# Three transformer blocks on one core: side stages at other positions, and the last changes of line by halves of the tokens

## The reference, cut to what matters

```python
def third_block(x, c, w_ada, b_ada, norm1_g, w_in, ..., w_out, norm2_g, w_ff1, w_ff2, final_g):
    ...
        xn = modulate(rmsnorm(h, norm1_g[l]), sh1, sc1)
        p = xn @ w_in[l]
        y_a = gmlp_branch(...)                  # token mixing, 8 groups
        y_b = mlstm_branch(...)                 # 4 heads of 256, called the memory here
        merged = sigmoid(p[GA]) * y_a + sigmoid(p[GB]) * y_b
        h = h + g1[:, None, :] * (merged @ w_out[l])
        xn = modulate(rmsnorm(h, norm2_g[l]), sh2, sc2)
        ff = jnp.square(jax.nn.relu(xn @ w_ff1[l])) @ w_ff2[l]      # 1024 -> 4096 -> 1024
        h = h + g2[:, None, :] * ff
    return rmsnorm(h, final_g)
```

## Time and profile before

| what | value |
|---|---|
| median of 3 runs (lowest, highest) | 2628.07 us (2627.79, 2630.12) |
| the profiled execution: its time | 2626.06 us |
| its span in the trace | 2624.2 us |
| TensorE busy | 2519.7 us (96%), 15220 matmuls |
| VectorE busy | 1540.4 us (59%) |
| ScalarE busy | 1084.1 us (41%) |
| GpSimd busy | 328.2 us (13%) |
| granted TensorE clock, mean | 0.991 |

### The profile page before, as it was taken

How to read it: one execution, slowest core, us unless ns; L and a number is a source line. 1 busy time by engine, 2 the same in 40 slices (tenths; PEclk the granted TensorE clock), 3 DMA queues, 4 the chain that set the end, 5 groups by cost and what they waited for, 6 DMA issues and landing times.

```text
span 2624.2 us, 37785 instructions
## 1 busy us (share of the span) xinstructions
PE 2519.7 (96%) x15220; PEld 2077.0 (79%) x15220; DVE 1540.4 (59%) x2544; ACT 1084.1 (41%) x1949; POOL 328.2 (13%) x225
## 2 busy tenths in 40 slices
PE   8889899999999999999899999999999999999998
PEld 6778898999998877766577777878866777699886
DVE  4987754654445457476647787454744544676444
ACT  4465454543223253235642223254333333466323
POOL 0143210012222010000012222020000000500001
PEclk9999999999999999999999999999999999999999
DMA  4211122222323341520035664332221123233332
GB/s 172 85 54 49 57 65 65 81 89 89 95 90 89 97 145 49 175 74 2 1 105 188 206 195 134 96 105 88 81 73 56 49 89 96 73 105 105 99 95 72
DMA packets 76987, 244.91 MB, mean 93 GB/s; under 512 B 12708, under 2 KB 18213, under 8 KB 76558
## 3 DMA queue, kind: packets, MB, share of 16 engines
q1 hardware_dynamic: 69470, 215.72, 26.6%
q10 hardware_dynamic: 7344, 26.77, 3.1%
HBM read 238.25 MB, written 6.90 MB: 93 GB/s over the span
## 4 chain that ended last, share of the span: by engine, by line
PE 78%; DVE 12%; ACT 5%; issue 3%; POOL 2%; DMA 0%; SPq 0%; ACTq 0%; DVEq 0%; POOLq 0%
PE ps L659 51%; PE ps L2525 8%; PE ps L861 5%; DVE wl L392 2%; ACT wh L380 2%; PE ps L3252 2%; PE ps L3961 1%; PE ps L3052 1%; PE ps L2273 1%; DVE xl L1126 1%; PE ps L2301 1%; DVE arena L1527 1%; PE ps L2290 1%; DVE arena L3631 1%; PE ps L1231 1%
## 5 line engine op out<-in xcount | busy, mean ns | idle before, releaser
L659 PE MATMUL ps<-xh,wh 128*128 128x512 f32 (+1 forms) x2536 | 932.4, 383 | 23.7 <-DVE xl L1152 8.1
L659 PE MATMUL ps<-xl,wh 128*128 128x512 f32 (+1 forms) x2536 | 913.5, 376 | 0.0
L659 PE MATMUL ps<-xh,wl 128*128 128x512 f32 (+1 forms) x2536 | 909.6, 374 | 0.0
L392 DVE TENSOR_TENSOR wl<-ring,wh 128x1024 fp32r<-128x1024 f32 x362 | 461.7, 1276 | 483.8 <-ACT wh L380 483.0
L380 ACT ACTIVATE wh<-ring 128x1024 fp32r<-128x1024 f32 x360 | 380.4, 1057 | 822.3 <-PE ps L659 726.8
L659 PEld LDWEIGHTS ps<-xh,wh 128*128 128x128 f32 x2536 | 464.5, 189 | 143.9 <-issue 41.9
L659 PEld LDWEIGHTS ps<-xh,wl 128*128 128x128 f32 x2536 | 464.1, 190 | 89.1
L659 PEld LDWEIGHTS ps<-xl,wh 128*128 128x128 f32 x2536 | 463.1, 189 | 88.2 <-issue 5.5
L2525 PE MATMUL ps<-xh,wh 128*128 128x264 f32 (+1 forms) x816 | 254.2, 312 | 5.3 <-DVE xl L446 3.8
L1221 POOL TENSOR_TENSOR arena<-arena 128x512 f32<-128x512 f32 (+1 forms) x35 | 60.3, 1727 | 1557.9 <-ACT arena L1206 1557.9
L2525 PE MATMUL ps<-xl,wh 128*128 128x264 f32 (+1 forms) x816 | 233.6, 286 | 0.0
(11 more groups left out here) (424 smaller groups left out, 3203.8 us busy)
## 6 DMA issues: line engine op xcount, KB each, us to landing
ring<-in_weights SPq DMA_DIRECT2D x374, 512.0 KB, 3.6
arena<-in_w_ada ACTq DMA_DIRECT2D x48, 512.0 KB, 4.5
arena<-in_cmp_w SPq DMA_DIRECT2D x2, 2048.0 KB
strip_copies<-strip_scratch SPq DMA_DIRECT2D x8, 327.5 KB, 6.3
arena<-strip_copies SPq DMA_DIRECT2D x8, 264.0 KB, 4.0
out_features<-arena SPq DMA_DIRECT2D x8, 256.0 KB, 2.1
token_scratch<-arena SPq DMA_DIRECT2D x3, 512.0 KB, 6.4
arena<-token_scratch SPq DMA_DIRECT2D x12, 128.0 KB, 4.0
```

What stands on the lines that cost most here:

```text
L392: dve.tensor_tensor(flat(self.wl[:, s % 2]), flat(self.ring[:, s % RING]), flat(self.wh[:, s % 2]).bitcast(F32), ALU.subtract).then_inc(se ...
L659: last = pe.matmul(self.place(u, e), w[:, k, :], x[:, k, o:o + m], start=(k == 0 and i == 0), stop=(k == self.chunks - 1 and i == 2))
```

## The change

It has two parts. The first gives other numbers to the positions of side stages in all three blocks, and nothing else: no instruction is added or taken away. The second is in block 3. The last two units (6 and 7) of the line behind `w_out` and of the last line are computed by halves of the tokens: first tokens 0 to 255 of both, then tokens 256 to 511 of both, the second half into another bank. `HalvedSums` makes the root for each half (squares of the last two chunks, ones, Ln and Exp by halves), `HalvedNorm` norms the first half while TensorE still works on the second, and the first two units of `Squared` (`opening`) go by halves too, unit 1 a few chunks behind unit 0. `Final` works and stores by halves: 16 operations and stores of 256 tokens instead of 8 of 512. `Squared` has eleven pairs instead of twelve, from unit 8 on instead of 6, and its planned start is 0.259 units behind the line before it, not 2.5.

Of the first part, three places of some fifty (the planner of block 1, and the memory):

```diff
-                    x.exp.append(x.mask[m] + 0.15 + 0.05 * m)
+                    x.exp.append(x.mask[m] + 0.167 + 0.05 * m)
...
                 free = x.keep[-1:] + [last.out for a in (1,) if s]
-                x.turned.append(max([x.turn + 0.27 * x.width * e, done + 0.15] + [a + 0.1 for a in free]))
+                x.turned.append(max([x.turn + 0.307 * x.width * e, done + 0.238] + [a + 0.048 for a in free]))
...
-            x.weigh = max(x.turn + 0.62 * x.width, x.keep[-1] + 0.12)
...
+            x.weigh = max(x.turn + 0.637 * x.width, x.keep[-1] + 0.116)
...
-        return self.at + 3 * (n // 4) + 0.6 * (n % 4)
+        return self.at + 2.8 * (n // 4) + 0.6 * (n % 4)
...
     memory = Memory(core, 31.2, QK[:, 0:NC], QK[:, NC:2 * NC], VT, EB, QK[:, 0:NC], PT, N, hsq, hr, conv, gates, tokens,
-                    (38, 40, 42.5, 45.3))
+                    (37.42, 40.3, 42.5, 45.13))
```

The second part:

```diff
-        if both:
+        end = self.n - 2 if self.halved else self.n
+        if self.opening:
+            for e in range(2):
+                lag = OPENING_LAG[e]
+                for k in range(NC + lag):
+                    if k < NC:
+                        yield 0, k, e
+                    if k >= lag:
+                        yield 1, k - lag, e
...
+        yield from [(u, k, None) for u in range(2 if both or self.opening else 0, end) for k in chunks if not self.paired(u)]
+        if self.halved:
+            yield from [(u, k, e) for e in range(2) for u in (self.n - 2, self.n - 1) for k in chunks]
...
+    def tensor(self, pe):
+        for e in range(2):
+            yield self.end(e) + (0.48 if e else 0.111)
+            got = self.core.ps[:, self.bank, e * HALF:e * HALF + HALF]
+            if e:
+                pe.wait_ge(self.root.sem, self.root.at(1))
+            for n, a in enumerate((self.acc, self.sq[:, (NC - 2) % 2], self.sq[:, (NC - 1) % 2])):
+                if n == 0:
+                    pe.wait_ge(self.added.sem, self.added.at(NC - 3))
+                else:
+                    pe.wait_ge(self.squared.sem, self.squared.at(NC - 2 + 2 * e + n))
+                last = pe.matmul(got, self.core.c("ones"), a[:, e * HALF:e * HALF + HALF], start=(n == 0), stop=(n == 2))
+            last.then_inc(self.summed.sem, 1)
...
+    def vector(self, dve):
+        for e in range(2):
+            a = self.half(e)
+
+            def part(k):
+                dve.wait_ge(self.hi.sem, self.hi.at(NC * e + k + 1))
+                dve.scalar_tensor_tensor(out=self.core.xl[:, k, a], in0=self.kept[:, k, a], scalar=self.shifts[k],
+                                         in1=self.core.xh[:, k, a].bitcast(F32), op0=ALU.add, op1=ALU.subtract).then_inc(self.lo.sem, 1)
+            for k in range(NC):
+                yield self.begin[e] + 0.145 * k
+                if k == 0:
+                    dve.wait_ge(self.sums.root.sem, self.sums.root.at(e + 1))
+                if k >= 2:
+                    part(k - 2)
+                dve.scalar_tensor_tensor(out=self.kept[:, k, a], in0=self.tiles[k][:, a], scalar=self.gains[k], in1=self.sums.r[:, a],
+                                         op0=ALU.mult, op1=ALU.mult).then_inc(self.made.sem, 1)
...
+            yield self.begin[1] + 0.145 * (k + 2) + 0.2
+            pool.wait_ge(self.lo.sem, self.lo.at(NC + k + 1))
+            pool.tensor_scalar(self.kept[:, k], self.kept[:, k], self.shifts[k], None, ALU.add).then_inc(self.shifted.sem, 1)
...
     def vector(self, dve):
-        yield self.sums.end() + 1
-        dve.wait_ge(self.sums.root.sem, self.sums.root.at(1))
-        for k in range(NC):
-            dve.scalar_tensor_tensor(out=self.final[:, k], in0=self.tiles[k], scalar=self.gains[k], in1=self.sums.r,
-                                     op0=ALU.mult, op1=ALU.mult).then_inc(self.made.sem, 1)
+        for e in range(2):
+            a = slice(e * HALF, e * HALF + HALF)
+            for k in range(NC):
+                yield self.sums.end(e) + 0.543 + 0.001 * k
+                if k == 0:
+                    dve.wait_ge(self.sums.root.sem, self.sums.root.at(e + 1))
+                dve.scalar_tensor_tensor(out=self.final[:, k, a], in0=self.tiles[k][:, a], scalar=self.gains[k], in1=self.sums.r[:, a],
+                                         op0=ALU.mult, op1=ALU.mult).then_inc(self.made.sem, 1)
...
+    def vector_half(self, dve, u, e):
+        dve.wait_ge(*((self.core.used, self.first + u + 1) if e else (self.half.sem, self.half.at(u - NC + 3))))
+        a = slice(e * HALF, e * HALF + HALF)
+        out = self.tiles[u][:, a]
+        dve.scalar_tensor_tensor(out=out, in0=self.place_half(u, e), scalar=self.scale[u], in1=out, op0=ALU.mult,
+                                 op1=ALU.add).then_inc(self.free.sem, 1)
...
-    last = Added(core, at, WHOLE, four, inputs, NC, h, cols(2 * NC))
+    last = Added(core, at, WHOLE, four, inputs, NC, h, cols(2 * NC), halved=(0, 1))
     last.alone = NC // 2
-    sums = Sums(core, at, 1, h, last.ready, T, 4, tmp, norm, names)
-    inputs_2 = Normed(core, h, at + NC + 1.1, sums.root, norm, cols(4 * NC), cols(3 * NC), 0, columns_ready, core.area(2 * NC * T, NC, T))
-    at += NC + 2.5
+    sums = HalvedSums(core, last, h, 4, tmp, norm, names)
+    inputs_2 = HalvedNorm(core, h, (at + NC - 0.75, at + NC + 1.213), sums, cols(4 * NC), cols(3 * NC), core.area(2 * NC * T, NC, T))
+    at += NC + 0.259
     three = (0, 1, 2)
-    up = Squared(core, 4 * NC, at, three, inputs_2, hidden, (6, 12))
-    up.alone = 0
-    of_norm = Quadrants(core, at + 1.6, inputs_2.kept, inputs_2.ready, hi, lo, quarters(3 * NC * T, 4))
+    up = Squared(core, 4 * NC, at, three, inputs_2, hidden, (8, 11))
+    up.opening = True
+    of_norm = Quadrants(core, at + 2.944, inputs_2.kept, inputs_2.ready, hi, lo, quarters(3 * NC * T, 4), split=(0.787,0.733))
...
-    some, last, at = down(core, at + up.start(4 * NC), up, hidden, 4 * NC, h, three, cols(5 * NC), quadrants=quadrants)
-    sums = Sums(core, last.at, last.d, h, last.ready, T, 4, 0, core.area(3 * T, T), names, ends=last.ends())
+    some, last, at = down(core, at + up.start(4 * NC), up, hidden, 4 * NC, h, three, cols(5 * NC), quadrants=quadrants, halved=(2, 3))
+    sums = HalvedSums(core, last, h, 4, 0, core.area(3 * T, T), names)
```

More of the change, by code:

```diff
@@ L1422, in down @@
         inputs = Inputs(core, [hidden[:, g + k] for k in range(m)], at - last.d, SEQ, ready=ready)
-        before = Added(core, at, WHOLE, banks, inputs, m, tiles, scale, pairs)
+        before = Added(core, at, WHOLE, banks, inputs, m, tiles, scale, pairs, halved if g + NC >= n else ())
         stages += [inputs, before]
@@ L3964, in steps @@
         def steps():
-            yield self.when(0) - 0.35
+            yield self.when(0) - 0.41
             score(0)
```

253 lines of the change are left out of this document (175 added, 78 removed).

## The result

The changed kernel took 2600.09 us (median; 2596.42 to 2605.73), the kernel before 2629.1 on the same chip; the ratio is 0.9888 (95% interval 0.9874 to 0.9903), that is 29 us. The forecast was 2616, in a range from 2607 to 2624. It had the sign right and the term of the halves, and fell short by some 17 us of gain, nearly all of it from the moved positions. A second measurement (`e8_all_again`) gave 2599.46 and 0.9887 (0.9869 to 0.9904).

A forecast was written before the change was run, and what follows sets the result against it. TensorE, carrying 78% of the chain, was taken to bound the kernel. Positions 8.0 plus halves 3.8 saved 11.8 us from the profiled 2626.06, giving 2614.3; 2.0 for the median made 2616, range 2607 to 2624.

The forecast's parts named there:

- Part B: The halves in block 3: change of line, pairs and tail together save 3.8 us.
- rival 4: Block 3's halves: the weight load sets their pace, 0.188 us each, 20 us more, 2636 us; chance 0.02.
- 2.5 - 1.1 - 0.6 = 0.8: Block 3's lines: 2.5 us saved at the change of line, 1.1 lost by eleven pairs, 0.6 by splitting wholes.
- Part A: The moved positions in all three blocks: 3.5 + 1.0 + 3.5 = 8.0 us saved.
- 1.6 + 1.4 + 2.0 - 1.5 = 3.5: Block 1, us saved: weighing waits 1.6, sums of squares 1.4, turns 2.0, less 1.5 for lost cover in differential heads.
- "1.0" of block 2: Block 2's scan and attention steps: 1.0 us saved, bounds 4 saved and 3 lost.
- the 3.5 of the mixer: Block 3's mixer: masked-score waits 3.0 us and two short ones 1.1 saved, less 0.6 for new waits.
- Cover: Other TensorE matmuls between a side chain's start and the instruction needing its result, at 0.12 us per 256-column matmul.
- Rival 1: Larger gain: change-of-line clock 1.5 us, block 2 3 more, block 1 4 more; 2607.5 us; chance 0.2.
- Rival 2: Change of line gives nothing, VectorE bounding it before and after; 2620.5 us; chance 0.15.
- Rival 3: Moved positions give nothing, TensorE waiting at the next instruction instead; saving falls from 8 to 1, 2623 us; chance 0.1.
- Rival 5: Slower: side work ahead of weight splits on VectorE makes TensorE wait; 25 units with 1 us each give 2629; chance 0.02.

The follow-up runs named there:

- e5_planner: Only the new numbers of block 1's attention planner, the rest as in the kernel before; ratio 0.9997 (0.9982 to 1.0012).
- e13_means_diff: The kernel before with block 1's differential heads starting at 21.74, their value turns, and the three new numbers of the root means; ratio 0.9973.
- e6_starts: Block 1's new numbers without the planner's (key choice round, head starts, root means, value turns), against the kernel before; ratio 0.9981, 5.0 us faster.
- e1_block1: Only the position numbers of block 1 changed, the rest as in the kernel before; 2614.34 us, ratio 0.9939.
- e3_block3: Only the position numbers of block 3's mixer changed, the rest as in the kernel before; 2623.26 us, ratio 0.9972.
- round: Only the key choice's second round in block 1 moved, from 21.4 to 22.3, against the kernel before; ratio 1.0003 (0.9992 to 1.0014).
- differential heads: Only block 1's differential heads started at 21.74 instead of 22.0, with their value turns, against the kernel before; ratio 0.9996 (0.9987 to 1.0005).

## Why the prediction was wrong, step by step

**Part B was right.** It forecast 3.8 us and 4.0 came. Halves of 256 columns ran 0.119 apart (2225.48, 2225.60, 2225.72), so rival 4 is out. On the scale of the prediction (zero at the end of the first token half, here 2225.7) the root was there at 3.2 (forecast 2.9), and the two units' last matmul at 24.1 (24.9): unit 2 starts at 2251.30 behind a wait of 1.16, and the last matmul issued 0.3 us before that wait began.

```profile
2225.48 0.28 PE L690 MATMUL ps<-xl,wh 128*128 128x256 f32 x1
...
2225.93 0.49 DVE L1481 SCALAR_TENSOR_TENSOR h<-ps,mod,h 128x256 f32<-128x256 f32 x1 [2.37 <-PE ps L690]
...
2228.88 0.88 DVE L1373 SCALAR_TENSOR_TENSOR arena<-h,mod,arena 128x256 f32<-128x256 f32 x2 [2.47 <-ACT arena L1309]
...
2236.41 0.70 PE L1330 MATMUL ps<-arena,con 128*128 128x256 f32 x2 [0.31 <-ACT arena L1305]
...
2251.30 0.47 PE L690 MATMUL ps<-xh,wh 128*128 128x512 f32 x1 [1.16 <-DVE wl L392]
```

What the working did not have is that last wait, for the split of unit 2. ScalarE's part of it, L380, follows the end of unit 0. Before, it started at 2276.89 and unit 1's last matmul issued 2.3 us later, so most of the split lay under unit 1's rest; now it started at 2248.83 and unit 1's last matmul came 1.0 later. From the matmul at the end of the mixer (2144.6 before, 2118.9 after) to the last one of the lines (2611.7 and 2585.4) the changed kernel is 0.6 us shorter, where 2.5 - 1.1 - 0.6 = 0.8 was forecast. The tail from the last line matmul to the end of the span is 9.1 us (forecast 9.3), before it was 12.5:

```profile
2585.39 0.28 PE L690 MATMUL ps<-xh,wl 128*128 128x256 f32 x1
...
2585.71 0.48 DVE L1481 SCALAR_TENSOR_TENSOR h<-ps,mod,h 128x256 f32<-128x256 f32 x1 [0.37 <-PE ps L690]
...
2588.45 3.26 DVE L1445 SCALAR_TENSOR_TENSOR arena<-h,par,arena 128x256 f32<-128x256 f32 x8 [2.25 <-ACT arena L1309]
```

**Part A was forecast at a third of what it gave.** The failing step is the sum of block 1, "1.6 + 1.4 + 2.0 - 1.5 = 3.5", measured at 16; with it the "1.0" of block 2 (5.5), and in size the 3.5 of the mixer (7.4). In the two profiles block 1's 14.6 us are 4.6 from 105.8 to 145.8 (forecast: nothing), 6.4 from 247 to 303 (about 3), 0.1 from 303 to 379 (a loss of 1.5) and 3.6 from 379 to 494 (2.0). What was wrong in them:

- "Up to 210 us the order hardly moves, so the rest of the 40.9 stays." It moved, on ScalarE's queue. From 105.8 to 145.8 two waits of TensorE went, one of 2.13 at 137.14 for ScalarE's root (L2907) and most of one of 1.08 at 132.33 for the eviction L3196. The root stood behind the exp L3187 of an attention step, which waited 3.02 us for its mask:

```profile
135.57 0.57 DVE L3135 TENSOR_TENSOR arena<-arena 128x400 f32<-128x400 f32 x1
136.18 0.54 ACT L3187 ACTIVATE arena<-arena 128x400 f32<-128x400 f32 x1 [3.02 <-DVE arena L3135]
136.63 0.46 ACT L2907 ACTIVATE arena<-ps,con 128x264 f32<-128x264 f32 x1
137.14 0.71 PE L2896 MATMUL ps<-arena,con 128*128 128x264 f32 x2 [2.13 <-ACT arena L2907]
```

With the planner's numbers alone (`e5_planner`) the root stands ahead of that exp, and the stretch is 35.4 us long, as in the changed kernel; with the root means' numbers and without the planner's (`e13_means_diff`, `e6_starts`) the wait stays, 2.13 and 2.30:

```profile
133.57 0.48 ACT L2907 ACTIVATE arena<-ps,con 128x264 f32<-128x264 f32 x1 [1.23 <-PE ps L2896]
134.88 0.54 ACT L3187 ACTIVATE arena<-arena 128x400 f32<-128x400 f32 x1 [0.83 <-DVE arena L3135]
```

- Cover was counted on TensorE alone, each wait by itself, with the chain behind it as long as before. The wait at 285.43 shows what this misses: its cause stood on VectorE's queue, two steps ahead, and with the order of masks and root means there changed it went as a whole. Of the 5.1 us less idle from 247 to 303 the weighing L3084 makes 2.7, L3052's wait for the mask L3120, which the sum left out, 1.2, and the sums of squares L2896 0.9, where the sum had 1.4.
- The loss of 1.5 that I took off for lost cover in the third and fourth differential heads was there only without the starts (76.0 to 77.2 with the planner's numbers alone, and with the soft heads' scores added); with the planner and all the starts it was 75.9. That the chain starts earlier would explain it; this was not followed row by row.
- In the mixer all waits went, not only the two of 3.0: 0.9 at L3990 as well, which I did not count; and no new ones came, for which I had taken 0.6. Which of block 3's numbers did what was not tried one by one. The row-order reading of L4012 was right: it ran at 1997.80, ahead of L392 at 1999.26, and L4135 (before L3961) ran with no wait.

```profile
1997.80 0.68 DVE L4186 SCALAR_TENSOR_TENSOR arena<-ps,arena 128x512 f32<-128x512 f32 x1
...
1998.91 1.02 PE L4135 MATMUL ps<-arena,con 128*128 128x512 f32 x2
1999.26 1.21 DVE L392 TENSOR_TENSOR wl<-ring,wh 128x1024 fp32r<-128x1024 f32 x1
```

- Each row's idle time leaves out the tail of the matmul ahead of it. At 285.43 the row says 1.90, and the matmul ahead of it issued at 283.25, 2.06 us more than the usual spacing of 0.12. With some 0.2 for each of six waits the mixer's are 1.2 us more than their rows (an estimate), and the sum left that out.
- **The clock.** From 105.8 to 145.8 TensorE had 0.93 of its full clock, with matmuls at the lower level behind the wait of 2.13 us; in the changed kernel's profiled execution it had 1.00 there. The prediction had a term for this at the change of line alone. Of the 14.6 us of block 1 from 105.8 to 494.2, 10.7 are idle time and 3.9 less busy time for the same matmuls: 2.4 in this stretch, the rest in stretches whose clock was 1.00 in both, where the tails ahead of the waits that went are the likely part (not shown).

How much of this is chance can be read from the repeated executions: a second profile of the changed kernel had 0.91 in that same stretch, which was 37.9 us long instead of 35.4. Over 114 executions of the kernel before and some 170 of the others, one slope fits all kernels: 1.8 us for each 0.001 of mean granted clock, with 1.3 us of scatter around it (least squares, one offset for each kernel). The kernel before ranged from 2622.5 us at 0.992 to 2636.2 at 0.986. At equal clock the whole change is 25.5 us faster, block 1's numbers 13.1, block 2's 3.9, block 3's 7.0, and the halves 0.1. This split is an arithmetical one, since the clock is itself a result of where TensorE idles, and for the halves the traces show that it misleads: their 4.0 us stand in every profile, whatever its clock. At the change of line the granted clock was 0.96 over 42.3 us in `before` and 0.92 in `e1_block1` (by that TensorE was at its lower level, 1.2 GHz, for some 3.4 and 6.8 us), and the stretch was equally long, so the lower clock cost nothing there:

```profile
2257.70:2300.00 42.30, 36.38 (x142) 0.96 0.21 63
```
```profile
2246.80:2289.10 42.30, 36.51 (x142) 0.92 0.22 63
```

With the halves the clock was 1.00 over the change of line (2225.7 to 2251.3). That raises the mean clock, and the slope counts that as time. So of the 5 us by which the whole is smaller at equal clock, some may be such a result of the change and not chance; how much is not shown.

**The profiled execution.** The prediction set everything against one execution, which took 388.4 us for the six stretches of block 1. Of five others with the same code there, three took 392.1, one 393.3 and one 388.6; in the side-only stretch of block 2 executions with the same code there took between 145.7 us (clock 0.98) and 152.8 (0.93). The profiled execution of before was thus on the short side in block 1, by up to 4 us, and so was that of the changed kernel: 373.8, where its second profile took 377.5. The execution of `e3_block3` shows the slower case (0.97 in the stretch from 249.2 where the one of before had 1.00, and 57.7 us for 56.2):

```profile
105.90:146.90 41.00, 32.86 (x226) 0.92 0.15 43
...
249.20:306.90 57.70, 49.44 (x351) 0.97 0.15 47
...
1175.20:1328.00 152.80, 133.91 (x1596) 0.93 0.02 5
```

**The signs.** Of those named for "right", these came: no wait for the masked scores and 5.4 us less idle in the mixer's stretch (3 forecast), 0.4 us of waits at the weighing, halves 0.119 apart, the ones at 10.7 behind a wait of 0.31, 9.1 us for the tail. The new line's first matmul came at 7.0 on that scale, straight behind the old line's last, and not at 3 to 4; the prediction's own account has the old line run to 6.4. One sign named for "wrong" came too: a half operation above 0.5 us on VectorE, the sixteen L1373 taking 0.54 in the mean. It did no harm to the forecast, which had set 24.9 for such a case and not the 23.6 of undisturbed halves.

**The rivals.** Rival 1 (larger, chance 0.2) is what happened, mostly in the places it named, but its 4 us more in block 1 were far too few (12 came), and its 1.5 for the clock at the change of line did not come, as the two stretches of 42.3 show. Rival 2 fell (the change of line gave what was forecast). Rival 3 is true of single numbers (round, differential heads, planner alone) and false of the whole. Rival 5 has one case in it: 1.16 us for a split at the new line's unit 2. The range failed since it took the bounds of each term from the same way of counting that was wrong.

## What to carry to other kernels

When positions are moved, count what is upstream: for each wait of the bounding engine go back over the queues of all engines to the operation that was late, and look how that operation's place moves; cover on the bounding engine alone gave less than a quarter of block 1's gain here. Take the idle time of a stretch, not the sum over known waits, as the measure of what a new order can give (18 of block 1's 26 idle us lay in the three stretches that got shorter, and 9.5 of them went), and add the tails: the last of the three had 2.2 us idle and got 3.6 shorter. Test sets of numbers together: five of the parts tried alone here gave nothing that could be measured or a loss, and four of these, each with another part, 4 to 16 us. And where a part's gain is small, look for the stretch that only this part touches: the halves' 3.4 us (1.3 to 5.8) by the whole time are 4.0 in every trace.

## What the runs showed of the hardware

- Executions of the kernel before differ by 13 us (0.5%), those of the planner alone by 21, with the granted TensorE clock, 1.8 us for 0.001. A large part of it falls in stretches where TensorE waits often and briefly: the side-only stretch had 0.93 to 0.98 with the same order, and took 152.8 to 145.7 us. It cost nothing where TensorE was waiting for another engine anyway (42.3 us at 0.96 and at 0.92).
- VectorE's L3147 (two inputs and one output in SBUF) took 0.37 us for 128x144 with POOL idle and 1.34 for the same shape while POOL's L2885 ran. The slow one ended 0.16 us behind L2885. The halved norm L1373 took 0.48 us with POOL idle; of the five that started under POOL's L1383, three took 0.82 or 0.83 and two 0.47 or 0.48. The Trainium skill ("SBUF — State Buffer", section "SBUF: two separate sides") says that such an operation and a GpSimd one keep each other off a shared port pair, if the GpSimd one reads SBUF, the second waiting for the first to end. L3147 agrees with this; the two L1373 that took 0.47 or 0.48 under POOL's shifts are left unexplained.
- A matmul of 256 columns cost TensorE half of one of 512, within 3% (one each 0.119 and 0.231 us), though its weight load shows 0.19. The Trainium skill ("TensorE: Matmul & The Clock Gate", section "Back-to-back issue gap") lets load and matmul set the spacing together; no row here shows the load setting it at this width.
